# Second block of a two-block model: transposed tiles waited for in pairs, a layer norm folded into columns, gating by chunks of z, squares about a first mean

## The chip, the cores and the metric

The kernel runs on one core of a Trainium2 chip. Its engines are TensorE (PE; PEld is its weight load), VectorE (DVE), ScalarE (ACT), GpSimd (POOL) and SyncE (SP, which here only issues transfers). The metric is the device time of one execution in microseconds (us); lower is better. A measurement of this kernel can tell about 0.3% from no change.

## What is computed

256 tokens of width 2048 go through two blocks, all in float32. The first block (attention and a linear recurrence, then a gather of 128 expert rows for each token) is not touched. The second block runs an even layer and an odd layer. Cut to what matters here:

```
# even layer, on the 256 latent tokens
xm  = x * (1 + sc0) + sh0                     # sc, sh, g: from the condition vector ("ada")
q, k, v, o, z_m, gates, u_p, z_p = split(xm @ w_in_even)
h   = mlstm(...);  h = normalize_per_head(h * sigmoid(o)) * mh_norm_g
y   = concat(h * silu(z_m), pooled_projection(u_p) * pool_scale * silu(z_p))
x   = layer_norm(ALPHA * x + g0 * (y @ w_out_even), post_ln_g[0], post_ln_b[0])
# odd layer
xm  = x * (1 + sc1) + sh1
u, v, z = split(xm @ w_in_odd)
v   = layer_norm(v, ln_g, ln_b);  s = einsum(w_sp, v) + b_sp
y   = u * s * silu(z)
out = layer_norm(ALPHA * x + g1 * (y @ w_out_odd), post_ln_g[1], post_ln_b[1])
```

## The kernel before

Every engine has its own instruction list, in the order in which the code writes it; semaphores join them. Nothing is rescheduled.

**A product** of the second block runs by chunks of 512 output columns. To keep float32 precision, each operand is held as a high part (`hi`, fp32r) and a rest (`lo`), and three products are summed: hi·hi, hi·lo, lo·hi. A chunk's weights come in four ring slots of 1 MB (`RING` = 4, filled by SyncE in the order of `plan.loads`), each holding two **pieces**. For piece j of a chunk ScalarE writes the high part (`split_hi`, L1113), VectorE the rest (`split_lo`, L1608; GpSimd for four of the latent products, L637), and TensorE multiplies it with two of the sixteen k tiles of the activations (`split_chunk`, L737). There are four piece buffers (`PIECES`), so piece n can be split only when TensorE has finished piece n-4. SyncE reloads a slot once the rests of its two pieces are written. Between the pieces VectorE takes the rows of the condition's matrix, one product with a sum of 2048 wide each (`ada_dots`, L1594), at the places that `ADA_AT` names; they go through the same ring.

**Activations** come to TensorE transposed. `transposes` (L778) turns four tiles into one PSUM bank, eight banks (units 0 to 7) for 256 x 2048. ScalarE empties the even units (L1090, high part L1095), with GpSimd writing their rest (L622); VectorE empties the odd units and writes both parts (L1568 or L1570, L1576, L1577). `wait_split` lets TensorE start the next product only when all eight units are done, on each of the three engines (in `w_even`, the first product after the even layer, four are wanted at once and the other four at its fifth piece).

**The order of the second block** is: `x2T` (transposes of x), the latent products `l_q` ... `l_z` with the mLSTM between, `yT` (its first four units before the last latent chunk, its last four after it), `gb0` (the gate g0 laid out as rows by 16 small matmuls), `w_even` in 4 chunks, the norm, `x3T`, `odd` in 12 chunks (4 of v, 4 of u, 4 of z), `sp` (16 matmuls with w_sp), the gating with z, `y3T`, `gb1`, `w_odd` in 4 chunks, the norm, the stores.

**The norm** after `w_even` and `w_odd` is in `post`: for each of 8 units VectorE multiplies by the gate (L2211), adds the old x (L2214) and sums (L2215); after the last it forms the means, subtracts them and multiplies by the gain (L2219) while ScalarE sums the squares about the mean (L1333); then the reciprocal root by 13 small operations (L1529 to L1536), and scale and bias (L2224). SyncE or TensorE can take x3 from there. Gating with z (L2264) and with w_sp's result (L2271) takes the whole of u at once.

Only these waits of TensorE are quoted, since the steps turn on them:

```
            pe.wait_ge(sem("x3_ready"), 2 * TT)
            transposes("x3T", KD, lambda k, tt: x3[:, tt, k * P:(k + 1) * P])
            wait_split("x3T")
            split_gemm("odd", 12, LO_ODD)
```

## Time and profile before

| | us |
|---|---|
| median of 3 runs | 2789.03 (2786.63 to 2793.39) |
| the profiled execution, its own time | 2789.35 |
| span of its trace | 2787.6 |
| second block, from x2T's transposes to the end | 951.6 (from 1836.0) |

The profile is of one execution. Its page gives, for each engine, how long it was busy; other views cut the span into stretches, follow the chain of waits that ended last back through the engines, or list single instructions in time. Times in them are microseconds from the start of the span. The "granted clock" (PEclk) is the share of its full clock (2.4 GHz) that TensorE was given: 0.5 is the lower of its two levels (1.2 GHz), and a value between is a stretch with some of both. An engine can be idle without harm if it isn't the one that the others wait for.

### The profile page before, as it was taken

How to read it: one execution, taken by the hardware profiler on the slowest of the kernel's cores; microseconds unless marked ns; L12 is line 12 of the kernel's file. 1: busy time of each engine (PE TensorE's matmuls, PEld its weight loads, DVE VectorE, ACT ScalarE, POOL GpSimd, SP SyncE). 2: the span in 40 equal slices, each digit the busy share in tenths (PEclk: the TensorE clock that was granted, in tenths of full speed). 3: DMA queues.
4: the chain of work that ended last, by engine and by line, in shares of the span. 5: the costliest groups of instructions: out<-in, count | busy, mean ns of one | idle time of the engine just before them, and what ended most of it. 6: DMA issues, size and time to landing. Idle time of an engine off the chain costs nothing.

```text
span 2787.6 us, 20533 instructions
## 1 busy us (share of the span) xinstructions
PE 1959.1 (70%) x7600; PEld 1343.7 (48%) x7600; DVE 1981.2 (71%) x2461; ACT 561.5 (20%) x804; POOL 1049.5 (38%) x648
## 2 busy tenths in 40 slices
PE   6999999789003777777775000059899898899987
PEld 3867448674001222222222000059788776688865
DVE  6786865977997666444446999989554968667566
ACT  2043100011000000100001000023433343445432
POOL 0011001264687555444545888810165620000000
...
GB/s 342 255 269 86 308 265 258 389 400 422 409 422 422 422 421 421 421 421 422 421 422 422 421 422 421 422 225 286 287 147 140 136 259 269 230 294 283 211 138 104
DMA packets 123507, 887.56 MB, mean 318 GB/s; under 512 B 13840, under 2 KB 14352, under 8 KB 16528
## 3 DMA queue, kind: packets, MB, share of 16 engines
...
## 4 chain that ended last, share of the span: by engine, by line
PE 39%; DMA 24%; POOL 15%; DVE 14%; issue 6%; ACT 1%; DVEq 0%; ACTq 0%; SPq 0%; POOLq 0%
PE psum L737 23%; DMA W<-in_peer_v,W 15%; POOL W L611 9%; POOL early_rows L611 6%; PE psum L679 6%; PE psum L703 4%; DMA early_rows<-in_peer_u,W 3%; PE psum L909 3%; DMA W<-in_peer_u,W 3%; DMA early_rows<-in_peer_v,W 2%; PE psum L954 1%; DMA XN<-in_ada 1%; PE psum L778 1%; DVE split L1608 1%; DVE W L1934 1%
## 5 line engine op out<-in xcount | busy, mean ns | idle before, releaser
L737 PE MATMUL psum<-split,hi 128*128 128x512 f32 x1664 | 521.0, 395 | 26.4 <-DVE split L1608 19.2
L1934 DVE CUSTOM_DVE_ANT_0 W<-W,XN 128x2048 f32<-128x2048 f32 x150 | 340.7, 2291 | 212.4 <-DMA W<-in_peer_u,W 211.6
L909 PE MATMUL psum<-W,HT 128*128 128x512 f32 x624 | 289.9, 609 | 276.6 <-ACT HT L1314 182.4
L1113 ACT ACTIVATE split<-ring 128x1024 fp32r<-128x1024 f32 x272 | 283.0, 1057 | 428.3 <-PE psum L737 333.6
L737 PEld LDWEIGHTS psum<-split,hi 128*128 128x128 f32 x1664 | 316.4, 191 | 94.3 <-issue 23.4
L1608 DVE TENSOR_TENSOR split<-ring,split 128x1024 fp32r<-128x1024 f32 x208 | 250.7, 1223 | 151.0 <-ACT split L1113 150.2
L1934 DVE CUSTOM_DVE_ANT_0 early_rows<-early_rows,XN 128x2048 f32<-128x2048 f32 x106 | 241.2, 2292 | 139.3 <-DMA early_rows<-in_peer_u,W 138.2
L611 POOL DMA_INDIRECT W<-in_peer_v,W x154 | 277.4, 1801 | 163.9 <-PE psum L909 134.8
L909 PEld LDWEIGHTS psum<-W,HT 128*128 128x128 f32 x624 | 114.2, 192 | 452.0 <-issue 309.3
L703 PE MATMUL psum<-HT,ring 128*128 128x256 f32 x1280 | 280.2, 382 | 22.3 <-ACT HT L1278 22.3
L611 POOL DMA_INDIRECT W<-in_peer_u,W x150 | 220.6, 1471 | 170.4 <-DVE W L1934 80.0
L703 PEld LDWEIGHTS psum<-HT,ring 128*128 128x128 f32 x1280 | 244.9, 192 | 56.2 <-ACT HT L1278 22.5
L637 POOL TENSOR_TENSOR split<-ring,split 128x1024 fp32r<-128x1024 f32 x64 | 158.1, 2490 | 245.9 <-ACT split L1113 245.9
L778 PE MATMUL psum<-cst,X 128*128 128x128 f32 x64 | 11.3, 360 | 340.0 <-DVEq L2012 323.8
L909 PE MATMUL psum<-early_rows,HT 128*128 128x512 f32 x400 | 187.0, 611 | 66.8 <-DMA early_rows<-in_peer_v,W 66.8
L611 POOL DMA_INDIRECT early_rows<-in_peer_v,W x102 | 185.9, 1823 | 116.0 <-PE psum L909 92.3
L737 PE MATMUL psum<-split,lo_odd 128*128 128x512 f32 x512 | 200.6, 392 | 0.0
L2008 DVE SCALAR_TENSOR_TENSOR X<-W,X 128x2048 f32<-128x2048 f32 x76 | 178.7, 2351 | 10.7 <-DMA W<-in_peer_v,W 1.1
L611 POOL DMA_INDIRECT early_rows<-in_peer_u,W x106 | 144.7, 1365 | 99.2 <-DVE W L1934 71.2
L778 PEld LDWEIGHTS psum<-cst,X 128*128 128x128 f32 x64 | 10.9, 194 | 341.3 <-DVEq L2012 324.6
L1314 ACT ACTIVATE HT<-cst,W 128x128 f32<-128x128 f32 x128 | 51.0, 401 | 566.1 <-PE psum L909 566.1
L622 POOL TENSOR_TENSOR lo_odd<-W,hi 128x512 fp32r<-128x512 f32 x8 | 11.8, 1477 | 397.7 <-ACT hi L1095 397.6
...
## 6 DMA issues: line engine op xcount, KB each, us to landing
...
```

Of the source, the lines that this page charges most:

```text
L611: nc.gpsimd.indirect_dma_start(row, None, t["peer_" + table], bass.IndirectOffsetOnAxis(ap=EIDX[:, c:c + 1], axis=0),).then_inc(full, 16)
L637: nc.gpsimd.tensor_tensor(split[:, to + 1024:to + 2048], ring[:, at:at + 1024], split[:, to:to + 1024], ALU.subtract).then_inc(sem("lo_poo ...
L679: m = nc.tensor.matmul(o[tt][:, 0:width], lhs[:, k, tt * P:(tt + 1) * P], sl[:, kk * width:(kk + 1) * width], start=(k == 0), stop=(k == s ...
L703: m = nc.tensor.matmul(o[a][:, S * b:S * b + S], sl[:, kk * 512 + m4 * P:kk * 512 + m4 * P + P], rhs[:, k, :], start=(k == 0 and b == 0), ...
L737: m = nc.tensor.matmul(dst, lhs, rhs, start=(k == 0 and b == 0 and not (features and i % 2)), stop=(k == KD - 1 and b == 2 and not (featur ...
L778: m = nc.tensor.transpose(o[:, kk * S + tt * P:kk * S + (tt + 1) * P], src(2 * i + kk, tt), IDENT)
L909: m = nc.tensor.matmul(o[c], DIAG[j % DIAGS], row[:, 512 * c:512 * c + 512], start=(j == 0), stop=(j == P - 1))
L1113: A(split[:, 2048 * (n % PIECES):2048 * (n % PIECES) + 1024], ring[:, at:at + 1024], ACT.Copy)\
L1314: A(DIAG[j % DIAGS], IDENT, ACT.Copy, scale=PACT[:, j:j + 1]).then_inc(sem("diag_ready"), 1)
L1608: TT_(split[:, to + 1024:to + 2048], ring[:, at:at + 1024], split[:, to:to + 1024], ALU.subtract)\
L1934: V.tensor_tensor_reduce(out=row, in0=row, in1=xn3[:, tt, :], scale=1.0, scalar=0.0, op0=ALU.mult, op1=ALU.add, accum_out=PACT[:, c:c + 1])\
L2008: STT(x3[:, 1, :], row, PACT[:, P + j:P + j + 1], x3[:, 1, :], ALU.mult, ALU.add)\
```

## The change

- **Pairs waited for one by one.** `wait_split` is gone. The first chunk after a transposition waits, at piece j, for unit j alone (`unit_split`, for `x2T`, `yT`, `x3T`, `y3T`). VectorE and ScalarE write the first pieces between the units. For `y3T` and the second half of `yT` the transposes themselves stand inside a chunk.
- **Norm folded.** After `w_even`, x is only normalised (L2363 of after); gain and bias of the norm are folded with the scale and shift of the odd layer into 32 columns (`fold_norm`) and used where `x3T` leaves PSUM. The full-width gain and bias for the residual come later, in chunks 1 and 2 of `odd` (L2384, L2385).
- **Squares about a first mean.** The squares of the first 1536 columns are taken about those columns' mean, ahead of the last chunk's end, and corrected afterwards; the sum of the last 512 columns comes from ScalarE (`last_sums`) and from the sum output of the last gate product.
- **Gating by chunk of z.** `sp` moves from behind `odd` 11 to behind `odd` 9; each chunk of z multiplies its 512 columns of u and is turned at once.
- The condition's rows in `w_even` move from 3, 3, 3, 3 by chunk to 2, 4, 3, 3. The mLSTM's gain now waits for a semaphore that two transfers raise.

The diff, cut to its core:

```diff
-    ADA_AT["w_even", _c] = (1, 1, 1, 0)
+    ADA_AT["w_even", _c] = ((0, 0, 1, 1), (1, 1, 1, 1), (1, 1, 1, 0), (1, 1, 1, 0))[_c]
...
+            def unit_split(name, i):
+                if i % 2:
+                    pe.wait_ge(turned(name, "dve"), turned_before[name] + i // 2 + 1)
+                else:
+                    pe.wait_ge(turned(name, "act"), turned_before[name] + i // 2 + 1)
+                    pe.wait_ge(turned(name, "pool"), turned_before[name] + i // 2 + 1)
...
+                    if fresh is not None:
+                        unit_split(fresh, j)
...
+            def ym_turn():
+                pe.wait_ge(sem("y_ready"), 2)
+                transposes("yT", KD, y_src, first=4)
...
+            for i in range(8):
+                if i % 4 == 0:
+                    pe.wait_ge(sem("xhat_ready"), TT * (i // 4 + 1))
+                o = open_unit(("x3T", i))
...
+                                                x3[:, tt, k * P:(k + 1) * P], IDENT)
+                close(m, ("x3T", i))
+            split_chunk("odd", 0, HI, LO_ODD, False, fresh="x3T")
...
+            def y3_turn(c):
+                def turn():
+                    pe.wait_ge(sem("y3_ready"), c + 1)
+                    transposes("y3T", 4 * c + 4, lambda k, tt: U3[:, tt, k * P:(k + 1) * P], first=2 * c)
+                return turn
+            split_chunk("odd", 10, HI, LO_ODD, False)
+            y3_turn(0)()
+            y3_turn(1)()
             pe.wait_ge(sem("ada_dot"), GATE1_DOTS)
             gate_rows("gb1", 1)
-            wait_split("y3T")
...
+            split_chunk("w_odd", 0, HI_3, LO_3, False, fresh="y3T", between={3: y3_turn(3)})
+            for c in range(1, 4):
+                split_chunk("w_odd", c, HI_3, LO_3, False)
...
-                act.wait_ge(sem("ln_mean"), n)
+            for i in range(4):
+                split_T("x2T", scale=lambda k: ada_v[:, 0, 16 + k, 0:1], bias=lambda k: ada_v[:, 0, k, 0:1],
+                        units=(2 * i,))
+                split_hi("l_q", 0, i, i + 1)
...
+            def post_squares(n, junk):
+                act.wait_ge(sem("ln_mean"), 2 * n - 1)
+                for tt in range(TT):
+                    A(junk[tt][:, 0:1536], x3[:, tt, 0:1536], ACT.Square, bias=st(270 + tt), accum_out=st(272 + tt))\
+                        .then_inc(sem("ln_squares"), 1)
+                for tt in range(TT):
+                    act.wait_ge(sem("post_last"), TT * (n - 1) + tt + 1)
+                    A(junk[tt][:, 1536:2048], x3[:, tt, 1536:2048], ACT.Square, bias=st(270 + tt), accum_out=st(274 + tt))\
+                        .then_inc(sem("ln_squares"), 1)
...
+            def last_sums(junk):
+                for tt in range(TT):
+                    A(junk[:, 512 * tt:512 * tt + 512], x3[:, tt, 1536:2048], ACT.Copy, accum_out=st(276 + tt))\
+                        .then_inc(sem("last_sums"), 1)
...
+            act.dma_start(PSC, t["pool_s"].to_broadcast([P, 1024])).then_inc(sem("mhg_loaded"), 16)
...
+            split_hi("w_even", 0, 0, 3)
             z_chunk(1)
...
+                act.sem_inc(sem("gb_ready"), 1)
+            split_hi("w_even", 0, 3, 4)
+            act.wait_ge(sem("cond_loaded"), 64)
+            A(COND_LAT[1], COND_LAT[1], ACT.Silu).then_inc(sem("cond_ready"), 1)
+            split_T("yT", hi=HI_Y, whole=WHOLE_Y, units=(4, 6))
...
+            act.wait_ge(sem("xhat_ready"), 2 * TT)
+            act.dma_start(LNG, t["ln_g0"].to_broadcast([P, D])).then_inc(sem("ln_loaded"), 16)
+            act.dma_start(LNB, t["ln_b0"].to_broadcast([P, D])).then_inc(sem("ln_loaded"), 16)
+            act.dma_start(w(16384, 1024), t["w_sp"]).then_inc(sem("sl_loaded"), 16)
...
+            for i in range(4):
+                split_T("x2T", LO_EVEN, scale=lambda k: ada_v[:, 0, 16 + k, 0:1], bias=lambda k: ada_v[:, 0, k, 0:1],
+                        units=(2 * i + 1,))
+                if i == 0:
+                    split_lo("l_q", 0, first=0, last=2)
+                else:
+                    split_lo("l_q", 0, first=i + 1, last=i + 2)
+            split_lo("l_q", 0, first=5, last=8)
...
+            dve.wait_ge(sem("mhg_loaded"), 32)
...
-            dve.sem_inc(sem("ym_ready"), 1)
+                if c == 0:
+                    split_lo("w_even", 0, first=0, last=3)
+            dve.sem_inc(sem("y_ready"), 1)
+            split_lo("w_even", 0, first=3, last=4)
             split_T("yT", LO_Y, hi=HI_Y, whole=WHOLE_Y, units=(5, 7))
...
+                    if i == 6:
+                        seq(V.tensor_reduce(st(270, 2), st(264, 6).rearrange("p (t c) -> p t c", t=2), AX.X, ALU.add))
+                        seq(TS(st(278, 2), st(270, 2), 1.0 / (3 * D), None, ALU.mult))
+                        TS(st(270, 2), st(270, 2), -1.0 / 1536, None, ALU.mult).then_inc(sem("ln_mean"), 1)
+                        dve.wait_ge(sem("ln_mean"), 2 * n - 1)
+                        dve.wait_ge(sem("last_sums"), TT * n)
+                        early()
...
+                        dve.wait_ge(sem("gb_ready"), 4 * n)
+                    if c < 3:
+                        m = TT_(junk[:, 0:512], bank((name, i)), gb[:, a], ALU.mult)
+                        give(m, (name, i))
+                        gave(dve, (name, i))
+                        seq(STT(x3[:, tt, a], x3[:, tt, a], ALPHA, junk[:, 0:512], ALU.mult, ALU.add))
+                        seq(V.tensor_reduce(st(264 + 3 * tt + c), x3[:, tt, a], AX.X, ALU.add))
+                    else:
+                        m = V.tensor_tensor_reduce(out=junk[:, 512 * tt:512 * tt + 512], in0=bank((name, i)), in1=gb[:, a],
+                                                   scale=1.0, scalar=0.0, op0=ALU.mult, op1=ALU.add,
...
+            def post_rstd(n):
+                dve.wait_ge(sem("ln_squares"), 6 * n - 2)
+                seq(TT_(st(282, 2), st(272, 2), st(274, 2), ALU.add))
+                seq(STT(st(282, 2), st(282, 2), 1.0 / D, st(252, 2), ALU.mult, ALU.subtract))
+                rstd(st(282, 2), st(282, 2), 1, LN_EPS, 200)
...
+            def fold_norm():
+                dve.wait_ge(sem("ada_dot"), ADA1_DOTS)
+                sc, sh = ada_v[:, 1, 16:32, 0], ada_v[:, 1, 0:16, 0]
+                a, b = COLS["ln_g0"][0], COLS["ln_b0"][0]
+                seq(TT_(fold[:, 0:16], col[:, a:a + 16], sc, ALU.mult))
+                seq(TT_(fold[:, 16:32], col[:, b:b + 16], sc, ALU.mult))
+                TT_(fold[:, 16:32], fold[:, 16:32], sh, ALU.add).then_inc(sem("folded"), 1)
+                split_lo("odd", 0, first=0, last=3)
...
+            post("w_even", 1, GBC, w(8192, 1024), fold_norm)
+            post_rstd(1)
+            seq(TT_(st(280, 2), st(280, 2), st(282, 2), ALU.mult))
+            for a in (slice(0, D // 2), slice(D // 2, D)):
                 for tt in range(TT):
...
+                    TS(x3[:, tt, a], x3[:, tt, a], st(282 + tt), st(280 + tt), ALU.mult, ALU.add).then_inc(sem("xhat_ready"), 1)
...
+            def y_chunk(c):
+                a = slice(512 * c, 512 * c + 512)
+                dve.wait_ge(sem("z3_ready"), c + 1)
+                for tt in range(TT):
+                    m = TT_(U3[:, tt, a], U3[:, tt, a], Z3[c % 2][:, tt, :], ALU.mult)
+                    if tt == 0:
+                        seq(m)
+                m.then_inc(sem("y3_ready"), 1)
...
+            y_chunk(0)
+            split_lo("odd", 10, first=4, last=8)
+            y_chunk(1)
+            split_lo("odd", 11, first=0, last=4)
+            split_T("y3T", LO_3, hi=HI_3, units=(1,))
+            y_chunk(2)
+            split_T("y3T", LO_3, hi=HI_3, units=(3,))
+            split_lo("odd", 11, first=4, last=8)
+            split_lo("w_odd", 0, first=0, last=1)
+            split_T("y3T", LO_3, hi=HI_3, units=(5,))
+            split_lo("w_odd", 0, first=1, last=3)
+            y_chunk(3)
+            split_lo("w_odd", 0, first=3, last=6)
+            split_T("y3T", LO_3, hi=HI_3, units=(7,))
+            split_lo("w_odd", 0, first=6, last=8)
...
+            OUT = (XN[:, 0:2048], w(8192 + 1024, 2048))
+            for tt in range(TT):
+                STT(OUT[tt], x3[:, tt, :], st(280 + tt), LNG1, ALU.add, ALU.mult).then_inc(sem("ln_centred"), 1)
+            post_rstd(2)
```

What moves is shown at three places. In these rows L... is the line, then the operation, what it writes and reads, the tile, and the semaphores it waits for.

VectorE at `x2T`, before: the last of the four odd units (L1568 to L1577), then the rests of the first pieces of `l_q` (L1608) and a row of the condition (L1594).

```order
L1568 TENSOR_SCALAR W<-psum,ada 128x256 [waits bank_full6]
L1568 TENSOR_SCALAR W<-psum,ada 128x256 [waits dve_done]
L1576 CAST hi<-W 128x512 [waits bank_free6]
L1577 TENSOR_TENSOR lo_even<-W,hi 128x512 [waits dve_done]
L1608 TENSOR_TENSOR split<-ring,split 128x1024 [waits hi_ready,cond_ready]
L1608 TENSOR_TENSOR split<-ring,split 128x1024 [waits hi_ready]
L1594 ISA ring,ada<-ring,XN,col 128x2048 [waits slot_full1]
```

The same engine and place of after, from the first odd unit on:

```order
L1648 TENSOR_SCALAR W<-psum,ada 128x256 [waits row_used,bank_full0,cond_ready,ada_dot]
L1648 TENSOR_SCALAR W<-psum,ada 128x256 [waits dve_done]
L1656 CAST hi<-W 128x512 [waits bank_free0]
L1657 TENSOR_TENSOR lo_even<-W,hi 128x512 [waits dve_done]
L1688 TENSOR_TENSOR split<-ring,split 128x1024 [waits hi_ready] x2
L1674 ISA ring,ada<-ring,XN,col 128x2048 [waits slot_full1]
L1674 ISA ada 128x1
L1648 TENSOR_SCALAR W<-psum,ada 128x256 [waits bank_full2]
L1648 TENSOR_SCALAR W<-psum,ada 128x256 [waits dve_done]
L1656 CAST hi<-W 128x512 [waits bank_free2]
```

The first two pieces' rests and the condition's row now stand between the first and the second odd unit.

ScalarE behind the last chunk of `w_even`, before: both squares of 2048 columns, four transfers, the first even unit of `x3T`.

```order
L1333 ACTIVATE W,stat<-X,stat 128x2048 [waits ln_mean]
L1333 ACTIVATE W,stat<-X,stat 128x2048 [waits ln_squares]
L1466 DMA W<-in_w_sp 128x1024 [waits x3_ready]
L1467 DMA W<-in_cond 128x2048
L1468 DMA W<-in_sgu_g 128x2048
L1469 DMA W<-in_sgu_b 128x2048
L1090 ACTIVATE W<-psum,ada 128x256 [waits bank_full1,ada_dot]
```

The same place of after:

```order
L1379 ACTIVATE W,stat<-X,stat 128x1536 [waits ln_mean]
L1379 ACTIVATE XN,stat<-X,stat 128x1536
L1383 ACTIVATE W,stat<-X,stat 128x512 [waits post_last]
L1383 ACTIVATE XN,stat<-X,stat 128x512 [waits post_last]
L1526 DMA W<-in_ln_g 128x2048 [waits xhat_ready]
L1527 DMA W<-in_ln_b 128x2048
L1528 DMA W<-in_w_sp 128x1024
L1529 DMA W<-in_cond 128x2048
L1530 DMA W<-in_sgu_g 128x2048
L1531 DMA W<-in_sgu_b 128x2048
L1124 ACTIVATE W<-psum,fold 128x256 [waits bank_full1,folded]
```

The squares are cut at column 1536, and six transfers instead of four stand ahead of the first unit.

VectorE between `odd` and `w_odd`, before: gating of the whole of u (L2264), then with `sp` (L2271), behind all rests of `odd`.

```order
L1608 TENSOR_TENSOR split<-ring,split 128x1024 [waits hi_ready] x7
L2264 TENSOR_TENSOR W<-W 128x2048 [waits odd_ready]
L2264 TENSOR_TENSOR W<-W 128x2048 [waits dve_done]
L2271 SCALAR_TENSOR_TENSOR W<-psum,col,W 128x256 [waits bank_full1,dve_done]
L2271 SCALAR_TENSOR_TENSOR W<-psum,col,W 128x256 [waits dve_done]
```

After, the stretch in which the rests of `odd` 11 and `w_odd` 0 (L1688), the units of `y3T` (L1650 to L1657) and the last chunk of z (L2405) take turns:

```order
L1688 TENSOR_TENSOR split<-ring,split 128x1024 [waits hi_ready] x5
L1650 COPY W<-psum 128x256 [waits bank_full2]
L1650 COPY W<-psum 128x256 [waits dve_done]
L1656 CAST hi_54<-W 128x512 [waits bank_free2]
L1657 TENSOR_TENSOR lo_55<-W,hi_54 128x512 [waits dve_done]
L1688 TENSOR_TENSOR split<-ring,split 128x1024 [waits hi_ready] x2
L2405 TENSOR_TENSOR W<-W 128x512 [waits z3_ready]
L2405 TENSOR_TENSOR W<-W 128x512 [waits dve_done]
L1688 TENSOR_TENSOR split<-ring,split 128x1024 [waits hi_ready] x3
```

The product with `sp` has moved to behind the first four rests of `odd` 10, and u is gated 512 columns at a time.

## Rows read from the trace of the kernel before

**Rows 1.** The page: busy time, share of the span and instructions of each engine.

```profile
PE 1959.1 (70%) x7600; PEld 1343.7 (48%) x7600; DVE 1981.2 (71%) x2461; ACT 561.5 (20%) x804; POOL 1049.5 (38%) x648
```

**Rows 2.** Stretches: length; busy us of PE, PEld, DVE, ACT, POOL; PEclk, DMA, GB/s.

```profile
2257.00:2268.00 11.00, 7.29 (x50) 7.12 (x50) 7.78 (x12) 9.10 (x12) 2.98 (x2) 0.84 0.45 191
2268.00:2357.00 89.00, 89.00 (x383) 71.63 (x383) 75.34 (x73) 31.69 (x32) 0.00 (x0) 1.00 0.87 331
2357.00:2387.00 30.00, 6.66 (x35) 5.99 (x33) 26.70 (x45) 14.80 (x20) 5.93 (x4) 0.63 0.31 123
2387.00:2651.00 264.00, 263.90 (x1152) 218.12 (x1153) 162.24 (x146) 116.27 (x128) 0.00 (x0) 0.99 0.71 255
2651.00:2679.00 28.00, 15.80 (x97) 14.42 (x95) 23.14 (x35) 10.05 (x18) 5.85 (x4) 0.88 0.20 75
```

**Rows 3.** The chain that ended last, in time: start us, us, what.

```profile
1850.27 59.79 PE psum L737 x474
...
2267.79 89.14 PE psum L737 x381
...
2387.10 263.41 PE psum L737 x1149
...
2679.23 88.15 PE psum L737 x381
```

**Rows 4.** Single instructions of VectorE at x2T: start, us, engine and line, idle before.

```profile
1838.10 1.12 DVE L1568 TENSOR_SCALAR W<-psum,ada 128x256 f32<-128x256 f32 x2 [2.19 <-PE psum L778]
...
1848.91 2.35 DVE L1608 TENSOR_TENSOR split<-ring,split 128x1024 fp32r<-128x1024 f32 x2
```

**Rows 5.** Stretch of the first latent chunk, L737 alone: busy PE, PEld; PEclk, DMA, GB/s.

```profile
1850.27:1876.00 25.73, 25.73 (x192) 25.73 (x193) 0.88 0.85 313
```

**Rows 6.** Transfers issued between 2150 and 2182 us: KB, us to landing.

```profile
W<-in_mh_g ACTq DMA_DIRECT2D x1, 512.0 KB, 3.4
W<-in_pool_s ACTq DMA_DIRECT2D x1, 512.0 KB, 4.6
```

**Rows 7.** Instructions behind the last latent chunk, in time.

```profile
2259.39 3.49 PE L778 MATMUL psum<-cst,XN 128*128 128x128 f32 x16 [2.37 <-DVEq L2196]
...
2262.72 3.74 PE L964 MATMUL psum<-cst,ada 128*128 128x128 f32 x32
```

**Rows 8.** Instructions between w_even and odd, in time.

```profile
2368.88 4.87 DVE L2224 SCALAR_TENSOR_TENSOR X<-W,stat 128x1024 f32<-128x1024 f32 x4
...
2375.81 1.16 ACT L1090 ACTIVATE W<-psum,ada 128x256 f32<-128x256 f32 x2 [9.82 <-PE psum L778]
...
2377.72 3.09 POOL L622 TENSOR_TENSOR lo_odd<-W,hi 128x512 fp32r<-128x512 f32 x2 [112.21 <-ACT hi L1095]
```

**Rows 9.** VectorE by line and shape: count, busy us, mean ns, idle before.

```profile
L1608 DVE TENSOR_TENSOR split<-ring,split 128x1024 fp32r<-128x1024 f32 x208 | 250.7, 1223 | 151.0 <-ACT split L1113 150.2
...
L1594 DVE CUSTOM_DVE_ANT_0 ring<-ring,XN,col 128x2048 f32<-128x2048 f32 x32 | 75.1, 2348 | 11.8 <-DMA ring<-in_ada 10.8 <-DVE W L1951 0.7
...
L2214 DVE SCALAR_TENSOR_TENSOR X<-X,W 128x512 f32<-128x512 f32 x16 | 11.1, 692 | 0.5
...
L2224 DVE SCALAR_TENSOR_TENSOR X<-W,stat 128x1024 f32<-128x1024 f32 x6 | 7.4, 1281 | 0.1
...
L1811 DVE TENSOR_SCALAR W<-W,stat 128x1024 f32<-128x1024 f32 x2 | 1.4, 752 | 0.0
```

**Rows 10.** Granted clock (third from the end) around three restarts of TensorE.

```profile
1845.00:1848.00 3.00, 0.00 (x0) 0.00 (x0) 2.84 (x6) 3.00 (x4) 0.76 (x1) 0.69 0.00 0
...
2380.00:2383.00 3.00, 0.00 (x0) 0.00 (x0) 2.90 (x5) 2.89 (x6) 2.07 (x2) 0.84 1.02 429
...
2679.00:2681.00 2.00, 1.77 (x4) 1.50 (x5) 2.00 (x3) 0.00 (x0) 0.00 (x0) 0.50 0.00 0
```

**Rows 11.** Between odd and w_odd: the matmuls with w_sp, and gating with them.

```profile
2651.01 7.07 PE L1040 MATMUL psum<-W 128*128 128x256 f32 x32
...
2656.60 9.05 DVE L2271 SCALAR_TENSOR_TENSOR W<-psum,col,W 128x256 f32<-128x256 f32 x16
```

**Rows 12.** ScalarE's table loads of one line, and the last of the norm's sums.

```profile
L1350 ACT ACT_TABLE_LOAD x3 | 3.8, 1283 | 13.5 <-PE psum L954 13.4
...
2361.77 2.00 ACT L1333 ACTIVATE W<-X,stat 128x2048 f32<-128x2048 f32 x1 [14.26 <-DVE stat L2230]
```

302 lines of the change are left out of this document (160 added, 142 removed).

## The prediction

> **What bounds the kernel now.** I first read the busy times [rows 1]: no engine is near 100%, so the stretches have to be read one by one. The stretches of the second block [rows 2] show two kinds. In `w_even` and `odd` TensorE is busy throughout (89.0 of 89.0, 263.9 of 264.0 us), at a clock of 1.00 and 0.99. Between them stand stretches in which it is nearly idle: 2357 to 2387 (6.7 us busy of 30, clock 0.63) and 2651 to 2679 (15.8 of 28). The chain that ended last [rows 3] agrees: it runs through TensorE's L737 in long pieces, and what lies between these pieces is what the change is after. So the path is the sum of full-rate products and of gaps; each term below is a gap before against the gap after. The first block isn't touched and I let it cost what it did.
>
> Piece times I use: 264 us for 12 chunks less the slow start is 21.8 us a chunk, 2.73 us a piece (from 1149 matmuls in 263.41 [rows 3]). For `l_q`, whose matmuls are half as wide, the first chunk took 25.73 us at a mean clock of 0.88 [rows 5], so 22.8 at full clock, 2.85 a piece, and 2.9 were lost to the low level (1.2 GHz) at its start. A rest costs VectorE 1.2, a condition's row 2.35, of which 2.3 before the next can start, an operation 512 wide 0.7, and a scale-and-shift by columns 1024 wide 0.75, against 1.28 for the three-operand form [rows 9].
>
> **Place 1, x2T (saves 3.4).** Before, VectorE works off four units from 1838.1 to 1848.9, 2.7 each, and only then the rests; L737 starts at 1850.3 [rows 3, 4] and ends at 1876.0 [rows 5]. After, VectorE goes unit, rest, rest, row, unit, rest, unit, rest, row, unit, rest, rest, row, rest, rest. From 1838.1 the first unit ends at 1841.3 (GpSimd slows it) and the rests are there at 1842.5, 1844.1, 1850.2, 1853.8, 1859.8, 1861, 1864.6, 1865.8 (later units taken at 2.4). TensorE at 2.85 a piece ends the chunk at 1871.2: 4.8 earlier, if its clock stays up in the waits for pieces 2, 3 and 4 (2.0, 0.8 and 3.2 us); with the old loss of 2.9 it is 1.9. I take 3.4, the middle. The rows of the condition are now ahead of rests that TensorE needs: the reason that an early start at 1842.5 isn't 8 us.
>
> **Place 2, the mLSTM's gain (costs 1.4).** The wait for `mhg_loaded` now wants both transfers. The one that it needed landed after 3.4 us, the other, issued 0.4 later, after 4.6 [rows 6]: 1.6 later, less 0.1 to 0.2 for the wait's own delay. VectorE's chain behind it leads straight to yT's transposes, with nothing else on that engine to do, so all of it counts.
>
> **Place 3, second half of yT (costs 2.5).** Before, the transposes start at 2259.4, 2.4 after the last latent chunk, and `w_even` at 2267.8 [rows 3, 7], 8.4 later; at 2.8 a piece its fifth piece would start 22.0 us after that chunk's end. After, the gate's matmuls (3.7 [rows 7]) and four pieces (11.2) come first, so the transposes start at 15.0; the same 8.4 us of units and first rest follow, since both ScalarE and VectorE do two units each before the fifth piece. That gives 23.4, 1.4 later, and TensorE idles for 8.4 - 3.5 = 4.9 us. The granted level outlives the work, by 2 us in one stretch without work (0.84 of 3 us) and longer in another (0.69 in three us that began after 3 idle ones) [rows 10]. So the restart is as likely as not at the low level, for 2.3: half of it is 1.1.
>
> Behind it VectorE has no lead left. From there to the end of `w_even` it has 28 rests (33.6), 12 rows (27.2), six evacuations at 2.17 (13.0), and three rests of `odd` with small ones (4.4): 78.2, against 28 pieces at 2.8 = 78.4 on TensorE. By piece it comes 1 us ahead at the third chunk, after the four rows of the second, and 6 ahead at the end. I cost it at nothing; a slip of 1 to 3 us is in the range. Ring and transfers: 9 MB of slots in that time, at 331 GB/s before [rows 2], fit.
>
> **Place 4, the norm and x3T (saves 16.3).** Call T the end of unit 6, 2357.0. Before, `odd` starts at 2387.1, T + 30.1 [rows 3], and loses 2.4 more to the low clock. After:
> - last two units: two operations instead of three each, 0.75 + 0.72 twice: T + 3.2 (VectorE is 0.2 late from the rests of `odd`);
> - means: four small ones at 0.2: T + 4.0. The squares are no longer 4.4 us in a row: those of 1536 columns (1.7 each, from 2.0 + 0.2 for 2048 [rows 12]) start when piece `odd` 2 is split, T - 1.7, and the last of 512 ends at T + 4.0;
> - root: 15 small ones and one product, 3.2: T + 7.2. Then four of 0.75 [rows 9], where 4.87 stood [rows 8]: halves ready at T + 8.7 and T + 10.2. The product of 4.6 us with gain is gone;
> - ScalarE issues six transfers instead of four before its first unit. Four took 2.06 (from 2373.75 to 2375.81 [rows 8]), six take 2.9 or so: first unit from T + 13.0, high part at T + 14.8, GpSimd's rest (1.3) T + 16.2. TensorE's 32 transposes are done by T + 14.8.
> So `odd` starts at T + 16.2. The rests 3 to 7, each behind a unit of VectorE, are there at 24.3 (with its unit), 25.5, 28.9, 32.3 and 33.5, against TensorE's wants of 24.4, 27.1, 29.9, 32.6 and 35.3: just in time. With 1.4 us between transposes and first piece the clock stays up. Saved: 13.9 + 2.4.
> In chunks 1 and 2 VectorE has 4.7 us more (L2384, L2385): 9.6 + 4.6 + 4.7 = 18.9 of 21.8, hidden behind TensorE.
>
> **Place 5, odd to w_odd (saves 11.7).** Before: from 2651.0 to 2679.2, 28.2 [rows 3, 11], with 1.4 lost to the low clock afterwards (0.50 at 2679 to 2681 [rows 10]). VectorE gated for 4.6 + 9.05 us [rows 11] before the first transpose. After, TensorE has only its own work left there: 7.1 for w_sp [rows 11], 7.0 for 32 transposes and 3.7 for the gate [rows 7], 17.8. I followed VectorE, ScalarE and the four buffers by piece: each rest of `odd` 10, 11 and `w_odd` 0 is 0 to 8 us ahead of TensorE, tightest at the fifth piece of `w_odd` (0.2 late, behind unit 6). Saved 28.2 + 1.4 - 17.8 = 11.8, less 0.1.
>
> **Place 6, the end (saves 0.5).** Two sums of 0.7 fall away, four small operations of 0.2 come: the rest is the same chain.
>
> **The sum.** -3.4 + 1.4 + 2.5 - 16.3 - 11.7 - 0.5 = -28.0 on 2789.35 (span 2787.6 and 1.75 around it): 2761.3, and since the profiled execution is 0.3 above the median, **2761**.
>
> **A rule weighed.** ScalarE changes between Silu, Copy, Identity and Square more often after the change. The trace shows loads of tables of 1.28 us where it goes to Sigmoid or Silu from Exp [rows 12], and none where Square follows Silu and Copy. The Trainium skill, page "ScalarE: Activation LUTs", section "What ACT_TABLE_LOAD costs", puts every switch to a different set at 2.66 us. If Silu and Square or Identity were in different sets, the four chunks of z (eight switches) would cost some 21 us on ScalarE, 5 of them on the path; I go by the rows and count none.
>
> **Rivals.**
> 1. *The interleaving starves TensorE* (15%). VectorE's order is fixed, and at places 1, 4 and 5 a rest stands behind a unit that waits for a bank or for GpSimd. If each slips by 1.5 us, place 4 loses 6, place 5 loses 4 and place 1 gives nothing: 2774. For it: 0 to 1 us of slack in three places. Against: VectorE is busy 162 of 264 us in `odd` [rows 2].
> 2. *VectorE becomes the bound in `w_even`* (12%). 78.2 against 78.4 leaves nothing; with 5% more for waits it is 4 us, at the third chunk's start, and the evacuations before the norm are late by 2: 2767.
> 3. *Clock and lead better than feared* (13%). Place 1 gives 4.8 or more, place 3 keeps its clock: 2757 or below.
> 4. *Slower: the granted clock gives way* (2%). From 2268 to 2768 TensorE would have no gap. It held 0.99 over 264 us without one [rows 2]. If over the 480 us it were granted 0.93, they would take 31 us more: 2792, slower than before. It decides from a mean of 0.94 down. Nothing in the rows shows such a fall.
> 5. *The waits don't move* (3%): a unit's wait for GpSimd or for a bank holds piece 0 to the time of the last unit; only places 4's norm (6 us) and 5's gating (9) remain: 2776.
>
> The forecast itself, 2757 to 2766, has 55%. The range is to reach over rivals 1, 2 and 3, with the bounds of places 1 and 3: 2753 to 2775. Faster by over 0.3% (about what a measurement can tell from no change) means below 2780.7: 0.94; within 0.3%: 0.03; slower: 0.03.
>
> **What would show it.** Place 1: first L737 of `l_q` near 1842.5, its first chunk's end near 1872 to 1874. Place 2: the first product with OG 1.4 us later behind the issue of mh_g. Place 3: 23 to 26 us from the last latent chunk to the fifth piece. Place 4: 16 us from unit 6 to `odd`'s first matmul and no second of idling in that chunk. Place 5: no idle time over 1 us on TensorE between `odd` 9 and the last unit. Wrong would be idle times of TensorE released by VectorE's L1688 in these chunks, or a granted clock below 0.97 in `odd`.

## The result and the profile after

The changed kernel takes **2762.85 us** (median; 2760.93 to 2765.68) where the kernel before takes 2790.91: ratio 0.9902, 95% interval 0.9885 to 0.9919, so 27 us faster (23 to 32). The profiled execution took 2762.08 us with a span of 2760.3, the one before 2789.35 with 2787.6. The forecast was 2761 in a range of 2753 to 2775.

The page of the kernel after, answering [rows 1]. The totals hardly moved; what went is time between pieces of work.

```profile
PE 1955.9 (71%) x7600; PEld 1339.6 (49%) x7600; DVE 1984.1 (72%) x2487; ACT 564.3 (20%) x820; POOL 1049.6 (38%) x648
```

Stretches of after, with the columns of [rows 2] (length; busy us of PE, PEld, DVE, ACT, POOL; PEclk, DMA, GB/s). They are cut at x2T's first transpose, `l_q`'s first evacuation, the last matmul of the mLSTM's heads, yT's first transpose, the end of the last latent chunk, VectorE's first product on unit 6 of `w_even` (the last chunk has units 6 and 7), `odd`'s first matmul, the start of `sp` behind `odd` 9, and `w_odd`'s last matmul.

```profile
1834.34:1871.16 36.82, 30.08 (x220) 29.27 (x221) 29.83 (x32) 17.70 (x23) 6.74 (x4) 0.91 0.62 218
1871.16:2162.94 291.78, 283.49 (x1554) 244.05 (x1552) 188.62 (x263) 110.76 (x114) 95.45 (x40) 0.98 0.57 208
2162.94:2231.44 68.50, 57.24 (x258) 47.65 (x257) 62.53 (x55) 27.68 (x31) 51.70 (x20) 0.92 0.43 149
2231.44:2258.04 26.60, 26.60 (x115) 22.55 (x116) 9.81 (x13) 10.49 (x14) 14.21 (x7) 0.89 0.53 187
...
2258.04:2361.02 102.98, 97.36 (x432) 78.72 (x430) 84.17 (x91) 43.40 (x51) 3.04 (x2) 0.97 0.73 282
2361.02:2377.21 16.19, 5.78 (x32) 5.58 (x33) 11.03 (x35) 6.17 (x12) 1.26 (x1) 0.68 0.51 191
...
2377.20:2595.80 218.60, 218.52 (x961) 180.20 (x962) 158.93 (x147) 104.33 (x118) 3.89 (x3) 1.00 0.77 284
2595.80:2741.60 145.80, 144.95 (x672) 120.68 (x671) 90.71 (x107) 62.76 (x75) 5.90 (x4) 1.00 0.44 155
```

The last two rows answer the long pieces of [rows 3]: from `odd`'s first matmul to `w_odd`'s last, 364.4 us, TensorE is idle for 0.9 in all, at a clock of 1.00. The same cuts in both traces:

| stretch | before | after | difference | place, forecast |
|---|---|---|---|---|
| up to x2T's transposes | 1836.0 | 1834.3 | -1.7 | untouched |
| x2T to `l_q`'s first evacuation | 39.5 | 36.8 | -2.7 | 1: -3.4 |
| to the end of the mLSTM's heads | 290.2 | 291.8 | +1.6 | untouched |
| to yT's transposes | 67.5 | 68.5 | +1.0 | 2: +1.4 |
| yT's first half and l_z 1 | 23.9 | 26.6 | +2.7 | none |
| to unit 6 of `w_even` | 99.9 | 103.0 | +3.1 | 3: +2.5 |
| unit 6 to `odd` | 30.1 | 16.2 | -13.9 | 4: -13.9 |
| `odd` to the end of `w_odd` | 380.9 | 364.4 | -16.5 | 4's clock -2.4, 5: -11.7 |
| to the end | 19.5 | 18.7 | -0.8 | 6: -0.5 |

The sum is -27.2, with rounding the difference of the spans (27.3). Three rows carry what was not forecast at all (-1.7, +1.6, +2.7), and the row of place 5 is 2.4 beyond its forecasts. The experiments were chosen for these, and to take the two big gains apart. With each experiment's time its ratio to the kernel before is given; the changed kernel's is 0.9902. Intervals are some 0.3% wide, so for terms of a few us the traces decide. The scatter between traces lies largely ahead of the change: x2T's transposes start between 1833.5 and 1844.4 us in 14 traces, though up to there the kernels differ in almost nothing (32 more constant columns are loaded).

### The profile page after: what moved, and what is told of

Same layout as the page of the kernel before. It is cut to its first block, busy times and chain, and to the rows that moved or that the text cites. A ratio compares the mean times of both kernels' runs of the same rounds, so it can differ in the third digit from the quotient of the medians.

```text
span 2760.3 us, 20601 instructions
## 1 busy us (share of the span) xinstructions
PE 1955.9 (71%) x7600; PEld 1339.6 (49%) x7600; DVE 1984.1 (72%) x2487; ACT 564.3 (20%) x820; POOL 1049.6 (38%) x648
## 4 chain that ended last, share of the span: by engine, by line
PE 38%; DMA 25%; POOL 15%; DVE 14%; issue 6%; ACT 2%; ACTq 0%; DVEq 0%; SPq 0%; POOLq 0%
PE psum L761 21%; DMA W<-in_peer_v,W 15%; POOL W L629 9%; POOL early_rows L629 6%; PE psum L693 6%; PE psum L717 4%; DMA early_rows<-in_peer_u,W 3%; PE psum L922 3%; DMA W<-in_peer_u,W 3%; DMA early_rows<-in_peer_v,W 2%; DVE split L1688 1%; PE psum L966 1%; DVE ring L1674 1%; DMA XN<-in_ada 1%; PE psum L951 1%
## 5 line engine op out<-in xcount | busy, mean ns | idle before, releaser
L1688 DVE TENSOR_TENSOR split<-ring,split 128x1024 fp32r<-128x1024 f32 x208 | 252.2, 1234 | 146.0 <-ACT split L1147 144.8
L797 PE MATMUL psum<-cst,X 128*128 128x128 f32 x32 | 5.4, 350 | 323.7 <-DVEq L2093 323.7
L797 PEld LDWEIGHTS psum<-cst,X 128*128 128x128 f32 x32 | 5.2, 188 | 324.5 <-DVEq L2093 324.5
L922 PEld LDWEIGHTS psum<-early_rows,HT 128*128 128x128 f32 x400 | 73.1, 192 | 180.5 <-ACT HT L1348 100.5
L693 PE MATMUL psum<-ring,W 128*128 128x512 f32 x336 | 148.1, 603 | 2.9 <-DVEq L1770 2.9
```

The source lines that it names most:

```text
L693: m = nc.tensor.matmul(o[tt][:, 0:width], lhs[:, k, tt * P:(tt + 1) * P], sl[:, kk * width:(kk + 1) * width], start=(k == 0), stop=(k == s ...
L922: m = nc.tensor.matmul(o[c], DIAG[j % DIAGS], row[:, 512 * c:512 * c + 512], start=(j == 0), stop=(j == P - 1))
L1688: TT_(split[:, to + 1024:to + 2048], ring[:, at:at + 1024], split[:, to:to + 1024], ALU.subtract)\
```

## The experiments

**Place 5 put back.**

```diff
-            split_chunk("odd", 10, HI, LO_ODD, False)
-            y3_turn(0)()
-            y3_turn(1)()
+            pe.wait_ge(sem("y3_ready"), 8)
+            transposes("y3T", KD, lambda k, tt: U3[:, tt, k * P:(k + 1) * P])
             pe.wait_ge(sem("ada_dot"), GATE1_DOTS)
             gate_rows("gb1", 1)
-            split_chunk("odd", 11, HI, LO_ODD, False, between={5: y3_turn(2)})
-            split_chunk("w_odd", 0, HI_3, LO_3, False, fresh="y3T", between={3: y3_turn(3)})
+            wait_split("y3T")
+            split_chunk("w_odd", 0, HI_3, LO_3, False)
```

> The changed kernel with place 5 alone put back: odd 10 and 11 in a row, then VectorE's gating with the whole of z, the matmuls with w_sp, all eight transposes of y3T, all their units waited for, then w_odd. Nothing of the computation is left out. Theory A (place 5 is worth what the two traces differ by there, from the end of odd 9 to the end of w_odd: 160.0 before, 145.5 after): 14.5 us slower than the changed kernel, 2777 us, and that stretch is 160 us again. Theory B (my term was right and the other 2.8 us came from elsewhere): 11.7 us slower, 2774.5, stretch 157. Rival C (the interleaved order only moves the wait, and w_odd would give most of it back): under 8 us, below 2771.

Measured: 2779.74 us, ratio 0.9968 (0.9958 to 0.9978). From `odd`'s first matmul to `w_odd`'s last 379.9 us instead of 364.4; less ten chunks of `odd` (218.6) that is 161.3. Theory A, and 1 us over it. TensorE's instructions between `odd` and `w_odd` in this kernel:

```profile
2638.14 7.07 PE L1061 MATMUL psum<-W 128*128 128x256 f32 x32
2652.89 6.18 PE L788 MATMUL psum<-cst,W 128*128 128x128 f32 x32 [7.68 <-DVEq L2394]
2658.91 3.74 PE L973 MATMUL psum<-cst,ada 128*128 128x128 f32 x32
```

The 7.7 us ahead of the transposes are the gating. By these traces place 5 is worth 15 us, not 11.7.

**Transposes of yT's second half ahead of the pieces.**

```diff
             gate_rows("gb0", 0)
-            split_chunk("w_even", 0, HI_Y, LO_Y, False, fresh="yT", between={4: ym_turn})
+            ym_turn()
+            split_chunk("w_even", 0, HI_Y, LO_Y, False, fresh="yT")
```

> The changed kernel with one thing moved at place 3: on TensorE the transposes of the second half of yT stand behind the gate's rows and ahead of w_even 0's four first pieces, not behind them. The units are still waited for one by one. Nothing of the computation is left out. Theory A (the idle 5.4 us ahead of the fifth piece and the 2.6 us of low clock behind it come from transposes that stand too late: in the new place VectorE and ScalarE have four pieces, 11 us, to do their units in): no idle time over 0.5 us ahead of the fifth piece, 7 to 8 us faster than the changed kernel, 2755 us. Rival B (VectorE is the bound of w_even, 78.2 us of work against 78.4: the 8 us come back as waits for its rests in the second and third chunk): the stretch from the last latent chunk to the end of w_even, 102.9 us now, shrinks by 3 us or less, 2760, with idle times released by the rests of L1688. Rival C (the transposes then wait for the gating of z, which ends 2.4 us after the last latent chunk, at a low clock): 4 us, 2759.

Measured: 2753.12 us, ratio 0.9869 (0.9855 to 0.9884). Theory A. First the changed kernel's wait for the fifth piece, then the same stretch (last latent chunk to unit 6) of this kernel:

```profile
2272.55 1.91 PE L797 MATMUL psum<-cst,XN 128*128 128x128 f32 x16
2279.97 1.22 PE L761 MATMUL psum<-split,hi_y 128*128 128x512 f32 x2 [5.51 <-DVE split L1688]
```

```profile
2260.24:2355.05 94.81, 94.81 (x432) 77.08 (x430) 84.20 (x90) 43.74 (x51) 2.70 (x2) 1.00 0.80 306
```

94.8 us instead of 103.0, no idle time, clock 1.00. So VectorE (84.2 us busy) isn't the bound of `w_even`, even with TensorE at full rate. The 8 us were the start that came too late.

**A semaphore of its own for pool_s.**

```diff
-            act.dma_start(PSC, t["pool_s"].to_broadcast([P, 1024])).then_inc(sem("mhg_loaded"), 16)
+            act.dma_start(PSC, t["pool_s"].to_broadcast([P, 1024])).then_inc(sem("psc_loaded"), 16)
-            dve.wait_ge(sem("mhg_loaded"), 32)
+            dve.wait_ge(sem("mhg_loaded"), 16)
```

> The changed kernel with place 2 alone put back: pool_s has its own semaphore again, and the first product with mh_g waits for mh_g alone. Nothing of the computation is left out. Theory A (the shared semaphore costs 1.0 us, and its longer idle time, 3.41 against 3.00 us, is what dropped TensorE's clock for the first half of yT and l_z 1, 2.7 us): those two stretches are 3.7 us shorter, 2759 us. Theory B (the low clock there has nothing to do with the wait): 1.0 us shorter, transposes still 3.7 us and l_z 1 still 22.8. Rival C (no effect: mh_g lands as late as pool_s on this queue): 0.

Measured: 2758.67 us, ratio 0.9889 (0.9874 to 0.9903). VectorE's wait for the transfers shrinks from 3.9 us to 2.4, as forecast at place 2, but the stretch to yT went from 68.5 to 65.5, by 3.0, and yT with l_z 1 from 26.6 to 23.9. Theory A on the clock, with a wait worth more than either theory said. yT's transposes before, after and in this kernel:

```profile
2233.26 1.97 PE L778 MATMUL psum<-cst,XN 128*128 128x128 f32 x16 [3.00 <-DVEq L2189]
```

```profile
2231.44 3.67 PE L797 MATMUL psum<-cst,XN 128*128 128x128 f32 x16 [3.41 <-DVEq L2276]
```

```profile
2232.28 1.97 PE L797 MATMUL psum<-cst,XN 128*128 128x128 f32 x16 [0.39 <-DVEq L2276]
```

Idle times ahead of yT in all traces but that of the shortened subtractions come in two groups of steps: 0, 0.39, 0.59 and 3.00 where the wait is for mh_g alone (five traces), 3.41 and 5.7 where it is for both (eight). The jumps to 3.00 and to 5.7 are 2.3 to 2.6 us, about as long as one of GpSimd's subtractions. That made the next three runs.

**The kernel before with the shared semaphore alone, and the kernel before again.** The first has the diff above reversed.

> The kernel before with place 2 alone: pool_s raises the semaphore of mh_g, and the first product with mh_g waits for both. Nothing of the computation is left out. Theory A (VectorE's small operations stand behind GpSimd's subtractions of 2.4 to 2.7 us, so a later start of the chain costs the wait's own 1.0 to 1.4 us and, when it misses a gap between two of them, one subtraction more; and 3.4 us or more of idle TensorE ahead of yT costs low clock on top): idle time ahead of yT's transposes 3.4 or 5.7 instead of 0 to 3.0, yT and l_z 1 25.2 to 26.6 us instead of 23.9, together 3 to 7 us slower than before. Theory B (my term: the wait's difference alone): 1.4 us slower.

> The kernel before once more, unchanged, for a second trace of it. If the idle time ahead of yT is set by the phase between VectorE's chain and GpSimd's subtractions, it is one of 0, 0.4 and 3.0 us, the values seen so far wherever the product with mh_g waits for mh_g alone, with the stretch from the mLSTM's last matmul to yT at 65.0 to 67.6; if it is fixed for this kernel, 3.0 and 67.5 again. The mLSTM stretch is 290.2 or 291.8 us by whether TensorE's clock drops in the first head's scores.

Measured: with the shared semaphore 2796.73 us against 2790.5, ratio 1.0021 (1.0010 to 1.0032), 6 us slower. Its rows, the stretch to yT and yT with l_z 1, and the transposes:

```profile
2171.54:2240.09 68.55, 57.32 (x256) 47.74 (x256) 62.35 (x54) 27.68 (x31) 51.70 (x20) 0.92 0.44 149
2240.09:2266.78 26.69, 26.59 (x112) 22.16 (x112) 5.14 (x10) 7.42 (x12) 14.21 (x7) 0.89 0.47 170
...
2240.09 3.67 PE L778 MATMUL psum<-cst,XN 128*128 128x128 f32 x16 [3.40 <-DVEq L2189]
```

The kernel before again: 2789.25 us, 65.4 and 23.9 us, idle 0.6, close to one of the values named; its mLSTM stretch took 291.2 us, neither of the two values named. So 3.0 and 67.5 aren't fixed for this kernel, which speaks for the phase between VectorE's chain and GpSimd's subtractions. Both stretches together are 88.8 to 91.4 us in the five traces with the wait for mh_g alone, and 95.1 to 96.1 in the eight with the shared one: 6 us between the means.

**GpSimd's subtractions shortened.**

```diff
+                        n_ = 64 if (name, c) in (("l_zp", 1), ("l_z", 0), ("l_z", 1)) else 1024
-                        nc.gpsimd.tensor_tensor(split[:, to + 1024:to + 2048], ring[:, at:at + 1024],
-                                                split[:, to:to + 1024], ALU.subtract).then_inc(sem("lo_pool"), 1)
+                        nc.gpsimd.tensor_tensor(split[:, to + 1024:to + 1024 + n_], ring[:, at:at + n_],
+                                                split[:, to:to + n_], ALU.subtract).then_inc(sem("lo_pool"), 1)
```

> The changed kernel, but GpSimd's subtractions for l_zp 1, l_z 0 and l_z 1 are 64 columns wide instead of 1024: the low parts of the other columns of those weights are left out (old contents are used in their place). Everything else as changed. Theory A (VectorE's chain ahead of yT is long because its operations wait behind GpSimd's subtractions): VectorE's small operations of 128x4 take 0.2 us each there, at most 0.3 on average, instead of 0.5 to 2.3, its products of 1024 columns 1.2 instead of 2.3, and TensorE has no idle time ahead of yT, so that the stretch is 61 to 65 us with yT and l_z 1 at 23.9. Theory B (these operations are slow for a reason of their own): their times stay, and idle 3.4 to 5.7.

Measured: 2756.35 us; 61.8 us to yT, no idle time, 23.8 for yT and l_z 1. GpSimd in the changed kernel in that stretch (seven subtractions in a row, 2.8 us each), and VectorE by line and shape (count, busy us, mean ns):

```profile
2169.84 19.43 POOL L655 TENSOR_TENSOR split<-ring,split 128x1024 fp32r<-128x1024 f32 x7
```

```profile
L1612 DVE TENSOR_SCALAR stat<-stat 128x4 f32<-128x4 f32 x2 | 4.6, 2306 | 0.1
L1611 DVE TENSOR_SCALAR stat<-stat 128x4 int32<-128x4 int32 x2 | 4.6, 2299 | 0.1
...
L2259 DVE TENSOR_TENSOR W<-XN 128x1024 f32<-128x1024 f32 x2 | 4.5, 2264 | 0.1
...
L2260 DVE TENSOR_REDUCE stat<-W 128x4 f32<-128x1024 f32 x2 | 2.4, 1221 | 0.1
```

The same in this kernel, whose lines stand one further down:

```profile
L2260 DVE TENSOR_TENSOR W<-XN 128x1024 f32<-128x1024 f32 x2 | 2.5, 1226 | 0.1
...
L1612 DVE TENSOR_SCALAR stat<-stat 128x4 int32<-128x4 int32 x2 | 0.3, 170 | 0.1
L1613 DVE TENSOR_SCALAR stat<-stat 128x4 f32<-128x4 f32 x2 | 0.3, 170 | 0.1
```

An operation on four columns takes 0.17 us here and 2.3 in a row beside the long subtractions. VectorE is busy 28.5 us in that stretch, against 62.5 in the changed kernel: theory A, in every number, and with the shared semaphore still in place. The sum of 1024 columns, which has one operand, takes 1.22 in both. The changed kernel's own trace shows the same within one chain, since GpSimd's seven subtractions end at 2189.27:

```profile
2186.98 2.31 DVE L1612 TENSOR_SCALAR stat<-stat 128x4 f32<-128x4 f32 x1
2189.32 0.16 DVE L1614 TENSOR_TENSOR stat<-stat 128x4 f32<-128x4 f32 x1
```

**The rows of the condition later.**

```diff
+ADA_AT["l_q", 0], ADA_AT["l_v", 1] = (0, 0, 1, 1), (1, 1, 1, 1)
```

> The changed kernel with VectorE's rows of the condition at place 1 moved: l_q 0 has two, behind its sixth and eighth piece, where it had three, behind the second, fourth and sixth; the third stands in l_v 1. Nothing of the computation is left out. Theory A (the rows ahead of rests that TensorE needs cause the waits for the third to fifth piece, 2.75 + 0.2 + 2.5 us in the changed kernel, and the low clock behind them): from x2T's transposes to the end of the first latent unit 36.8 becomes 34 or less, 2 to 4 us less. Rival B (GpSimd's subtraction beside it, in which VectorE's rests take 1.7 us instead of 1.2, and the units themselves cause them): under 1 us less. Either way the time moves by too little for the timed runs alone, 2759 to 2762; the trace decides.

Measured: 2765.58 us, ratio 0.9903 (0.9887 to 0.9919). At x2T theory A, and more than it said: 29.9 us instead of 36.8, no wait for a rest over 0.2 us, clock 0.95 over the stretch where it was 0.91. The time didn't follow: the mLSTM stretch is 294.3 instead of 291.8 (TensorE waits 1.1 us for the gates in l_v 1, with a low clock behind it), and this trace starts x2T 10 us later than the changed kernel's.

**Place 1 put back.**

```diff
             transposes("x2T", KD, lambda k, tt: x3[:, tt, k * P:(k + 1) * P])
+            wait_split("x2T")
```

with ScalarE's and VectorE's units in a row and the rests behind them.

> The changed kernel with place 1 alone put back: x2T's eight units waited for together, VectorE's four units in a row, then rests and rows. Nothing of the computation is left out. Theory A (place 1 is worth 2.7 us, 39.5 against 36.8 from the transposes to the end of the first latent unit): that stretch is 39.5 again. Theory B (it also decides how late the low clock comes in the mLSTM stretch: 290.2 before, 291.8 after): with the old x2T the mLSTM stretch is 290.2 and the clock 1.00 in the first heads' scores. Rival C (the low clock there comes and goes from run to run): it is not tied to this edit.

Measured: 2765.52 us, ratio 0.9912 (0.9897 to 0.9928); x2T to the first evacuation 39.2 us. Theory A: 38.2 to 39.5 in the four traces with the old order, 35.5 to 37.0 in the seven with the new order and the rows where the change puts them; 3.2 us between the means. Theory B fell: the mLSTM stretch is 291.8 with the old x2T too. Over the 11 traces in which the rows of the condition were not moved it is between 290.0 and 292.0, in kernels of both kinds: rival C.

**All eight units of x3T waited for together.**

```diff
+            wait_split("x3T")
-            split_chunk("odd", 0, HI, LO_ODD, False, fresh="x3T")
+            split_chunk("odd", 0, HI, LO_ODD, False)
```

with VectorE's four units in a row.

> The changed kernel, but at x3T TensorE waits for all eight units before odd 0, and VectorE does its four units in a row, then the rests 3 to 7. Norm, fold and everything else as changed. Nothing of the computation is left out. Theory A (the waits one by one are worth the time in which VectorE does three further units, 2.4 to 2.7 each, less nothing, since behind them all goes at full rate in both): odd's first matmul 7 to 8 us later after the last unit of w_even (24 instead of 16.3), and the clock low for 2 us behind it: 8 to 10 us slower, 2771 us. Rival B (the rests 3 to 7 are then early, and in the changed kernel they were late, so part comes back within the chunk): 5 us or less, 2767.

Measured: 2772.8 us, ratio 0.9930 (0.9912 to 0.9948). Unit 6 to `odd`, and what follows:

```profile
2366.40:2388.20 21.80, 5.57 (x33) 5.29 (x33) 19.37 (x48) 10.71 (x19) 5.56 (x4) 0.78 0.64 251
2388.20:2400.00 11.80, 11.78 (x44) 9.63 (x45) 3.75 (x4) 3.18 (x3) 0.00 (x0) 0.83 0.55 211
```

5.6 us later than the changed kernel, plus 1.5 lost to the low clock behind it (ten chunks 220.1 against 218.6): 7.1. The size lies between the theories. That the wait for further units costs time and clock was right, but not whose units they are. The last instructions ahead of `odd` in this kernel:

```profile
2386.31 0.69 DVE L1664 TENSOR_TENSOR lo_odd<-W,hi 128x512 fp32r<-128x512 f32 x1
2386.40 1.73 POOL L640 TENSOR_TENSOR lo_odd<-W,hi 128x512 fp32r<-128x512 f32 x1 [0.45 <-ACT hi L1136]
...
2388.22 1.19 PE L761 MATMUL psum<-split,hi 128*128 128x512 f32 x2 [7.87 <-POOL lo_odd L640]
```

VectorE's fourth unit is done at 2387.0; TensorE starts behind GpSimd's rest of the last even unit, at 2388.1. ScalarE and GpSimd turn an even unit every 1.7 us, and three further ones are the larger part of the 5.6.

**One exact mean.**

```diff
-                    A(junk[tt][:, 0:1536], x3[:, tt, 0:1536], ACT.Square, bias=st(270 + tt), accum_out=st(272 + tt))\
+                    A(junk[tt], x3[:, tt, :], ACT.Square, bias=st(280 + tt), accum_out=st(272 + tt))\
```

> The changed kernel, but ScalarE squares all 2048 columns about the exact mean, behind the last unit, in both norms of the second block, instead of 1536 about a first mean ahead of it and 512 behind. The sums stay fused as changed. Nothing of the computation is left out. Theory A (squares 2.2 each, 4.4 us in a row, stand on the path of the first norm; in the last one they are hidden beside VectorE's two products of 2.35): 4.2 us slower, 2767 us, with odd's first matmul 20.5 after the last unit of w_even. Theory B (on both paths): 8 us, 2771. Rival C (hidden behind the issue of transfers and the transposes): under 1 us.

VectorE's sums and the waits are changed to match. Measured: 2766.14 us, ratio 0.9916 (0.9900 to 0.9932). Unit 6 to `odd` 20.2 us, 4.0 more; the end 18.3, 0.4 less. Theory A. ScalarE's squares in the first norm:

```profile
2361.05 2.00 ACT L1379 ACTIVATE W<-X,stat 128x2048 f32<-128x2048 f32 x1 [5.64 <-DVE stat L2321]
...
2363.05 1.99 ACT L1379 ACTIVATE XN<-X,stat 128x2048 f32<-128x2048 f32 x1
```

In the last norm they lie beside VectorE's two products: the first mean brings nothing there.

**Combined.** The transposes ahead of the pieces, the semaphore of its own and the rows later, together, then the same with the third row of the condition in l_k 1.

> The changed kernel with three edits: transposes of the second half of yT ahead of w_even's first pieces, a semaphore of its own for pool_s, and the rows of the condition later at x2T. Nothing of the computation is left out. If each gives what its theory A says (7.5, 1 to 3.7, 2 to 4), 11 to 14 us faster than the changed kernel, 2750 us; if VectorE bounds w_even and the clock is not tied to the wait, 4 to 5 us, 2758.

> As the combined kernel (transposes ahead of w_even's pieces, own semaphore for pool_s, rows of the condition later at x2T), but the third row stands in l_k 1 and not in l_v 1. Nothing of the computation is left out. Theory A (the row in l_v 1 makes VectorE 1 us late at the mLSTM's gates, an idle time of 0.9 to 1.1 and 3.4 to 6.8 us at low clock that the changed kernel has not or less of; l_k 1 has 3 us to spare): mLSTM stretch 290.2 to 291.8 instead of 292.6, idle ahead of L991 under 0.2 us, 1 to 2.5 us faster than the combined kernel, 2744. Rival (VectorE has no time to spare in l_k 1 either, and TensorE waits for a rest there): no gain.

Measured: 2746.27 us, ratio 0.9846 (0.9828 to 0.9865), and 2745.7 us, ratio 0.9831 (0.9813 to 0.9850). Both beat the changed kernel, by some 16 and 20 us by the ratios, each known to some 7 us; 11 to 14 were forecast for the first. The stretches of the first, in the order of the table (x2T, to yT, yT and l_z 1, to unit 6):

```profile
1838.44:1868.38 29.94, 28.82 (x220) 28.28 (x221) 26.35 (x31) 16.53 (x22) 6.85 (x4) 0.93 0.54 181
2160.97:2225.96 64.99, 57.04 (x257) 47.77 (x257) 58.77 (x55) 25.54 (x28) 47.90 (x18) 0.92 0.42 146
2225.96:2249.79 23.83, 23.83 (x116) 20.03 (x115) 20.95 (x13) 12.65 (x18) 18.94 (x9) 1.00 0.64 229
2249.79:2344.70 94.91, 94.81 (x432) 77.07 (x430) 84.47 (x91) 43.96 (x51) 2.68 (x2) 1.00 0.81 308
```

They add up: 6.9 + 3.5 + 2.8 + 8.1 = 21.3 us under the changed kernel's, less 0.8 in the mLSTM stretch and 4.1 by the later start of x2T; the spans differ by 16.4. Moving the row to l_k 1 removed the idle time of 0.9 us at the gates, but the low clock there stayed and the stretch is as long (292.5): no gain that can be told from none.

## Why the prediction was right, place by place

**Place 1** (forecast -3.4, measured -2.7; -3.2 by the means of the traces with either order). The reason given was right: rows of the condition ahead of rests. The first piece came at 1841.0 and the waits behind it were 2.75, 0.23 and 2.50 us where 2.0, 0.8 and 3.2 stood. The clock did drop, once, behind the last wait. The three rows of the condition were in the way: with them later, no wait over 0.2 us is left and the stretch is 29.9 us.

**Place 2** (forecast +1.4). Here a step failed. "1.6 later, less 0.1 to 0.2" was right for the wait itself (2.3 us before, 3.9 after), but it took VectorE's chain behind it to keep its length. It doesn't. Its operations stand behind GpSimd's subtractions, so it comes late by whole steps of these, and TensorE's longer idle time then costs clock. In these two traces it cost +1.0 and +2.7 (the row without a forecast); over 13 traces the means are 6.0 apart, and the timed runs of the kernel before with the shared semaphore alone say the same. The sign was there in the trace of before, where products of 1024 columns took 2.26 us in that stretch:

```profile
L2172 DVE TENSOR_TENSOR W<-XN 128x1024 f32<-128x1024 f32 x2 | 4.5, 2258 | 0.1
```

against 1.2 for a rest of the same size [rows 9].

**Place 3** (+2.5, measured +3.1). The two halves were off in opposite ways, and 0.7 of the row belongs to place 4 (below). Order: +1.4 forecast, +0.1 measured (22.0 us from the last latent chunk to the fifth piece against 21.9). The 8.4 us from transposes to piece were taken from [rows 7], where 16 transposes took 3.5 us at the low clock (0.52 in that stretch); at full clock they took 1.9. The 8.4 came out as 7.4, and the four pieces ahead were 0.4 shorter than forecast. Restart: +1.1 forecast as half of 2.3, and +2.6 measured, since it came in full:

```profile
2274.50:2280.00 5.50, 0.03 (x1) 0.03 (x1) 5.33 (x9) 5.22 (x8) 3.04 (x2) 0.84 0.00 0
2280.00:2284.00 4.00, 4.00 (x10) 3.13 (x11) 4.00 (x4) 0.00 (x0) 0.00 (x0) 0.50 0.48 127
```

Rival 2 (VectorE the bound of `w_even`) was wrong, as the second experiment shows.

**Place 4** (-16.3, of it -13.9 for the stretch and -2.4 for the clock; measured -13.2 to -13.9 and -2.0). The clock's part: `odd`'s 12 chunks took 263.9 us before, and 261.9 in the kernel with place 5 put back. For the stretch it matters where T stands. The table cuts at VectorE's first product on unit 6, and from there `odd` starts after 16.2 us. But in the changed kernel VectorE comes to that product late, straight from rests of `odd`:

```profile
2357.61 3.49 DVE L1688 TENSOR_TENSOR split<-ring,split 128x1024 fp32r<-128x1024 f32 x3
2361.02 0.68 DVE L2317 CUSTOM_DVE_ANT_0 W<-psum,W 128x512 f32<-128x512 f32 x1
```

Counted from `w_even`'s last matmul (2357.62 before, 2360.92 after) the stretch is 29.5 and 16.3: -13.2. So VectorE was some 0.8 us late where the forecast had 0.2, and from the end of unit 6 itself (in the trace of before 0.6 ahead of the last matmul) `odd` starts at about T + 17, not T + 16.2. The exact hit of the row is an effect of the cut. The parts, by experiment: 4.0 for the squares, 5.6 and 1.5 of clock for the waits one by one. The remaining 4.8 of 15.9 (gain and bias folded into columns, one product less) were not run alone.

**Place 5** (-11.7, measured -14.5, the row's -16.5 less 2.0 of place 4's clock; -15.5 by its experiment). The mechanism was right, a term was mis-sized: 7.0 us for 32 transposes, from two times 3.5 in [rows 7]. The row there was taken at a low clock, behind an idle time. At full clock:

```profile
2624.31 1.91 PE L797 MATMUL psum<-cst,W 128*128 128x128 f32 x16
```

So 3.8 instead of 7.0: 3.2 of gain more. Against it stands the one wait for a rest, ahead of `w_odd`'s fifth piece as forecast, which was 0.84 us and not 0.2.

**Place 6** (-0.5, measured -0.8): the same chain, as forecast.

**The rivals.** No clock below 0.97 in `odd` (rival 4), waits do move (rival 5), 0.9 us of idle time in 364 (rival 1 at place 5). Rival 3 didn't come: place 1 gave 2.7, and the clock dropped at place 3. The table loads that were weighed didn't come either: 25 in each of the two traces, none of them behind 2170 us. That the sum came within 2 us has two causes. Places 4 and 6 were near. The other is luck: places 2 and 5 were off by 2.3 and 2.8 us in opposite directions (at place 2 it is 4.6 by the means of the traces), and the -1.7 and +1.6 of the two untouched stretches cancel too. Both errors have one reason: a time was taken as fixed that something else stretches, GpSimd at place 2, the clock at place 5.

**What stays open.** Why the mLSTM stretch varies from 290.0 to 292.0. In the changed kernel the clock drops in the first head's scores (0.73 over 2031.1 to 2037.4), behind some 2 us of small matmuls (8x8 and 8x256) with under 0.2 us of idle time; the same code kept it at 1.00 in the kernel before. It isn't tied to the change: the kernel before with the shared semaphore has the drop too (0.69 over 2040.5 to 2046.0, stretch 292.0). Nor is it the whole of it: with the semaphore of its own the clock stayed at 1.00 there, and the stretch was 291.8.
